# Places of split weights counted among split units, next weights rounded ahead of the residual, and a new order of the mixers' first jobs

## What is computed

```python
for l in range(DEPTH):                      # 2
    x = x + 0.5 * swiglu(rms_norm(x, ffn1_norm[l]), ffn1_w_gate[l], ffn1_w_up[l], ffn1_w_down[l])
    h = rms_norm(x, mix_norm[l])
    (nq, nkc, nvc, ..., wq, wk, wv, bgate) = jnp.split(h @ w_in[l], SPLIT_POINTS, axis=-1)
    y_nsa = nsa_attention(...)              # 8 heads; compressed, selected and window keys
    y_sb = stick_breaking_attention(...)    # 4 heads
    y_swa = swa_sink_attention(...)         # 4 heads
    g = sigmoid(bgate).reshape(B, S, 3, D_MODEL)
    merged = (g[:, :, 0] * (y_nsa @ w_up_nsa[l]) + g[:, :, 1] * (y_sb @ w_up_sb[l])
              + g[:, :, 2] * (y_swa @ w_up_swa[l]))
    x = x + merged @ w_out[l]
    x = x + 0.5 * swiglu(rms_norm(x, ffn2_norm[l]), ffn2_w_gate[l], ffn2_w_up[l], ffn2_w_down[l])
```

## Time and profile before

| | us |
|---|---|
| median of 3 runs | 2611.62 (2607.24 to 2613.82) |
| profiled execution | 2605.64 |
| its span, first to last instruction | 2603.8 |
| PE busy | 2497.8 |
| DVE busy | 1629.0 |
| ACT busy | 1190.7 |
| POOL busy | 367.0 |
| mean granted TensorE clock, of full | 0.979 |

### The profile page before, as it was taken

The page is one execution under the profiler, slowest core; times in us unless marked ns, Lnnn a source line. Parts: engine busy times, 40 slices in busy tenths (PEclk is TensorE's granted clock), DMA queues, the critical chain, the costliest instruction groups (busy, mean ns, idle before and its releaser), DMA issues.

```text
span 2603.8 us, 42299 instructions
## 1 busy us (share of the span) xinstructions
PE 2497.8 (96%) x18041; PEld 2319.9 (89%) x18041; DVE 1629.0 (63%) x2438; ACT 1190.7 (46%) x1950; POOL 367.0 (14%) x385
## 2 busy tenths in 40 slices
PE   8999989999999999999999988999999999999998
PEld 7999978999999898899998655888888999999998
DVE  4787466777887865667774876542443654556753
ACT  5444456544344355555444543431332534344653
POOL 1311000332023000022331220200001011011000
PEclk9999899999999999999999999999999999999999
DMA  7667544567676766347775220233322423334552
GB/s 237 211 220 219 154 135 119 166 223 235 228 233 223 230 154 190 113 126 250 259 262 156 58 68 1 75 104 97 97 98 88 129 90 115 99 108 141 166 195 98
DMA packets 386385, 401.65 MB, mean 154 GB/s; under 512 B 44695, under 2 KB 370611, under 8 KB 385940
## 3 DMA queue, kind: packets, MB, share of 16 engines
q1 hardware_dynamic: 383448, 391.19, 48.1%
q10 hardware_dynamic: 2748, 7.76, 0.8%
HBM read 394.72 MB, written 4.19 MB: 153 GB/s over the span
## 4 chain that ended last, share of the span: by engine, by line
PE 74%; DVE 17%; ACT 5%; issue 2%; DMA 1%; POOL 1%; ACTq 0%; DVEq 0%; SPq 0%
PE bank L672 22%; PE bank L673 21%; PE bank L674 21%; DVE rounded L2332 6%; PE bank L680 3%; DVE plain L2321 3%; ACT rounded L1588 2%; PE bank L685 2%; PE bank L1524 1%; DVE plain L2579 1%; POOL plain L3379 1%; ACT plain L1778 1%; PE bank L1087 1%; PE bank L1117 0%; DVE plain L2456 0%
## 5 line engine op out<-in xcount | busy, mean ns | idle before, releaser
L672 PE MATMUL bank<-rounded 128*128 128x256 f32 (+1 forms) x3704 | 1120.4, 302 | 22.2 <-DVE rounded L2332 17.8
L673 PE MATMUL bank<-rounded 128*128 128x256 f32 (+1 forms) x3704 | 1102.4, 298 | 0.0
L674 PE MATMUL bank<-rounded 128*128 128x256 f32 (+1 forms) x3704 | 1101.7, 297 | 0.0
L2332 DVE TENSOR_TENSOR rounded<-plain,rounded 128x1024 fp32r<-128x1024 f32 (+1 forms) x618 | 722.6, 1216 | 518.9 <-ACT rounded L1588 518.7
L672 PEld LDWEIGHTS bank<-rounded 128*128 128x128 f32 x3704 | 717.5, 194 | 57.2 <-DVE rounded L2332 20.3
L1588 ACT ACTIVATE rounded<-plain 128x1024 fp32r<-128x1024 f32 (+1 forms) x630 | 616.8, 1032 | 327.9 <-PE bank L674 283.7
L673 PEld LDWEIGHTS bank<-rounded 128*128 128x128 f32 x3704 | 717.5, 194 | 16.4
L674 PEld LDWEIGHTS bank<-rounded 128*128 128x128 f32 x3704 | 717.1, 194 | 16.5
L672 PE MATMUL bank<-rounded,rounded 128*128 128x256 f32 (+2 forms) x1472 | 452.6, 307 | 19.9 <-DVE rounded L2332 16.5
L673 PE MATMUL bank<-rounded,rounded 128*128 128x256 f32 (+2 forms) x1472 | 449.9, 306 | 0.0
L674 PE MATMUL bank<-rounded,rounded 128*128 128x256 f32 (+2 forms) x1472 | 448.6, 305 | 0.0
(11 more groups left out here) (306 smaller groups left out, 1988.3 us busy)
## 6 DMA issues: line engine op xcount, KB each, us to landing
plain<-in_mlp_w SPq DMA_DIRECT2D x64, 1024.0 KB, 5.3
plain<-in_ada_w SPq DMA_DIRECT2D x48, 1024.0 KB, 5.4
plain<-in_ffn_w_gate SPq DMA_DIRECT2D x44, 1024.0 KB, 5.8
plain<-in_ffn_w_up SPq DMA_DIRECT2D x44, 1024.0 KB, 5.9
plain<-in_ffn_w_down SPq DMA_DIRECT2D x32, 1024.0 KB, 5.2
plain<-in_w_in SPq DMA_DIRECT2D x32, 1024.0 KB, 5.6
plain<-in_od_w_in SPq DMA_DIRECT2D x32, 1024.0 KB, 5.7
plain<-in_ffn_w_down SPq DMA_DIRECT2D x16, 768.0 KB, 5.1
```

What stands on the lines that cost most here:

```text
L672: pe.matmul(dst, a[0], b[0], start=first and i == 0, stop=False)
L673: pe.matmul(dst, a[0], b[1], start=False, stop=False)
L674: ins = pe.matmul(dst, a[1], b[0], start=False, stop=last and i == n - 1)
L2332: dve.tensor_tensor(low, raw, top, SUB).then_inc(*done(("lo", m, half)))
```

## The change

Three things. First, the split places are handed out by a unit's rank among split units (`split_turn`) and no longer by its number; so `before(m)` is the split unit three ranks back. The raw places stay at m % 3. Second, in the FFN's down projection ACT writes `hi` of the unit three ahead, and the modulation's fill, and DVE writes `lo`, ahead of the residual, its operand for the next product, and the squares. Third, in the mixer, PE's second gate product precedes the compressor's last part, the value product of the compressed branch goes behind gate 2, `third(i)` goes ahead of `compressed(0)`, ACT loads its Exp table by an activation on a spare element, takes job 0's weights ahead of gate 2 and of `headroot`; DVE does `then(0)` right after `first(0)`, `headnorm` after `first(1)`, the gate units' `lo` one iteration later; and the up-projection waits for the bank of the last attention output instead of DVE's mark `attended`, while the last `lo` (unit 71) stands behind that mark.

```diff
     def slot(self, m):
+        return SPLIT + 4096 * (self.split_turn[m] % AHEAD)
     def before(self, m):
-        m -= AHEAD
-        while m >= 0 and self.units[m][2] != "split":
-            m -= AHEAD
-        return m if m >= 0 else None
+        n = self.split_turn[m] - AHEAD
+        return self.split_units[n] if n >= 0 else None
...
         gate(0)
+        gate(1)
         compress(1, 1)
         keyfactors()
-        gate(1)
...
         scores(0)
         gate(2)
+        values_compressed()
         headsum("kc", 15)
...
                 scores(i + 1)
+            gate(4 + 2 * i)
+            third(i)
             if i == 0:
                 compressed(0)
-            gate(4 + 2 * i)
-            third(i)
...
-                for x in new(at(s, "attended", "dve")):
+                for x in new(at("free", s, "ao", n - 1)):
                     pe.wait_ge(*x)
...
         for x in range(12):
             blk, k0 = x // 3, 8 * (x % 3)
+            if x < 11:
+                hi(U[s, "d", blk, k0] + 3)
+                fill(s, 22 + x)
             if k0 == 16:
...
-            if x < 11:
-                hi(U[s, "d", blk, k0] + 3)
-                fill(s, 22 + x)
...
         gate(0)
+        gate(1)
         hidden(1)
-        gate(1)
         headsq("kc", M.bank(s, "kc")[:, 0:15], 15, ("kc",))
+        act.activation(M.spare, M.epsc, ACT.Exp, bias=0.0, scale=1.0).then_inc(*done())
...
+        weights(0)
         gate(2)
-        weights(0)
+        for x in new(at(s, "vc")):
+            act.wait_ge(*x)
+        act.activation(b_.vc[0:15, :, :], grid(M.bank(s, "vc")[0:15, 0:128], c=2), ACT.Copy, scale=1.0).then_inc(
+            *done((s, "vc", "s"), ("free", s, "vc")))
+        hi(U[s, "w1", 1, 1] + 3)
         headroot("kc", 15)
-        hi(U[s, "w1", 1, 1] + 3)
         gate(3)
...
             blk, k0 = x // 3, 8 * (x % 3)
+            if x < 11:
+                lo(U[s, "d", blk, k0] + 3)
             if k0 == 16:
...
             if x < 11:
-                lo(U[s, "d", blk, k0] + 3)
                 fill(s, 22 + x)
...
         first(0)
-        lo(U[s, "bg", 0] + 3)
         then(0)
-        headnorm("kc", b_.kc[:, 0:15], 15)
         lo(U[s, "w1", 1, 1] + 3)
-        lo(U[s, "bg", 1] + 3)
         for i in range(n):
             if i + 1 < n:
                 first(i + 1)
+                if i == 0:
+                    headnorm("kc", b_.kc[:, 0:15], 15)
                 then(i + 1)
+            else:
+                lo(U[s, "bg", 1 + i] + 3)
...
-            lo(U[s, "bg", 2 + i] + 3)
+            if i + 1 < n:
+                lo(U[s, "bg", 1 + i] + 3)
         here(s, "attended", "dve")
         for x in new(at(s, "attended", "pe"), at(s, "attended", "act"), L.last()):
             dve.wait_ge(*x)
+        lo(U[s, "bg", 11] + 3)
```

More of the change, by code:

```diff
@@ L231, in __init__ @@
         self.plan()
+        self.split_units = [m for m, u in enumerate(self.units) if u[2] == "split"]
+        self.split_turn = {m: n for n, m in enumerate(self.split_units)}
     def piece(self, tensors, o, n):
@@ L262, in part @@
     def part(self, m, k, c0, n=128):
-        o = SPLIT + 4096 * (m % AHEAD) + k * self.units[m][3] + c0
+        o = self.slot(m) + k * self.units[m][3] + c0
         return self.split_words(o, n), self.split_words(o + 2048, n)
@@ L269, in halves, with slot @@
     def halves(self, m):
-        width, raw, o = self.units[m][1], self.raw(m), SPLIT + 4096 * (m % AHEAD)
+        width, raw, o = self.units[m][1], self.raw(m), self.slot(m)
         for a, n in ((0, width // 2), (width // 2, width - width // 2)):
             yield raw[:, a:a + n], self.split_words(o + a, n), self.seen(o + a, n), self.split_words(o + 2048 + a, n)
+    def slot(self, m):
+        return SPLIT + 4096 * (self.split_turn[m] % AHEAD)
     def before(self, m):
-        m -= AHEAD
-        while m >= 0 and self.units[m][2] != "split":
-            m -= AHEAD
-        return m if m >= 0 else None
+        n = self.split_turn[m] - AHEAD
+        return self.split_units[n] if n >= 0 else None
     def is_split(self, m):
@@ L1041, in mixer, with values_compressed @@
         ins.then_inc(*done((s, "kc")))
-        b = bank(s, "vc")
-        for x in new(at(s, "hidT", 1, "s")):
-            pe.wait_ge(*x)
-        for g in range(2):
-            ins = plain(b[0:15, g * 64:g * 64 + 64],
-                        [(b_.hidT[1][:, c, g * 15:g * 15 + 15], v2[:, 2 + c, :]) for c in range(2)])
-        ins.then_inc(*done((s, "vc")))
+        def values_compressed():
+            b = bank(s, "vc")
+            for x in new(at(s, "hidT", 1, "s")):
+                pe.wait_ge(*x)
+            for g in range(2):
+                ins = plain(b[0:15, g * 64:g * 64 + 64],
+                            [(b_.hidT[1][:, c, g * 15:g * 15 + 15], v2[:, 2 + c, :]) for c in range(2)])
+            ins.then_inc(*done((s, "vc")))
         def compressed(step):
@@ L1915, in mixer @@
         gate(0)
+        gate(1)
         hidden(1)
-        gate(1)
         headsq("kc", M.bank(s, "kc")[:, 0:15], 15, ("kc",))
-        for x in new(at(s, "vc")):
-            act.wait_ge(*x)
-        act.activation(b_.vc[0:15, :, :], grid(M.bank(s, "vc")[0:15, 0:128], c=2), ACT.Copy, scale=1.0).then_inc(
-            *done((s, "vc", "s"), ("free", s, "vc")))
+        act.activation(M.spare, M.epsc, ACT.Exp, bias=0.0, scale=1.0).then_inc(*done())
         def compressed(step):
@@ L2754, in mixer @@
         lo(U[s, "va", 1] + 3)
+        lo(U[s, "bg", 0] + 3)
         hidden(1)
@@ L2806, in first @@
             n = 128 * (i + 1)
-            landed = [at(s, "vc"), at(s, "gk"), at(s, "T"), at(s, "rq")]
+            landed = [at(s, "cb", 1, 1), at(s, "gk"), at(s, "T"), at(s, "rq")]
             for g in range(2):
```

## The result

| | before | after |
|---|---|---|
| median | 2610.72 us (4 runs, 2607.24 to 2613.82) | 2580.76 us (4 runs, 2577.38 to 2581.84) |
| profiled execution's span | 2603.8 us | 2575.6 us |
| mean granted clock | 0.979 | 0.983 |

The ratio is 0.9885, 95% interval 0.9872 to 0.9897, so 30.0 us (27 to 33) less. The forecast was 2584 with a range of 2574 to 2599. The two spans differ by 28.2 us.

The account below looks back on a forecast made before the run. PE was taken to bound the kernel, with idle time, mostly waits for `lo`, and half clock left to win. Gains of 11.4 + 8 + 5.5 + 2.5 + 0.5 - 0.6 = 27.3 us off 2611.6 gave 2584, range 2574 to 2599.

Parts of the forecast that it names:

- Step 1: End of each mixer's attention: the first up-projection's stall goes, less a bank wait; gain 5.7 us per mixer.
- Step 2: First jobs of each mixer's attention: the new order shortens PE's waits and half clock; gain 4 us per mixer.
- (b): First jobs: `keyfactors` and compressed keys come later; the compressed scores' wait grows from 0.4 to about 1.6 us.
- (a): First jobs: early Exp table and direct `then(0)` ready job 0's weights sooner; waits of 0.89 and 0.4 us go.
- Step 3: Down projection in b0 and b1: `hi` and `lo` ahead of the residual; gain 5.5 and 2.5 us.
- Step 4: Down projection in a0 and a1: same reorder, paid back in bank waits; net -0.6 and +0.5 us.
- Step 5: Split places by rank: PE isn't waiting at the gate and up phase's holds; gain 0.
- A: FFN part gives nothing: b0's and b1's gains go in a0's and a1's bank waits; 2592 us, chance 0.13.
- B: First jobs: compressed keys and gated weights come too late, so that part gives nothing; 2592 us, chance 0.15.
- C: FFNs: residual behind `lo` makes PE wait for a bank at 12 steps; 2655 us, chance 0.03.
- D: b0's holds are by landing, not order, so only the attention-end gain remains; 2600 us, chance 0.09.
- E: Up-projection: `lo` slowed beside POOL's merges, 1.5 us more per mixer; 2587 us, chance 0.10.

Follow-up runs that it names:

- e4: Old kernel with only the up-projection waiting for the last attention output's free bank and the last `lo` behind DVE's mark: 2600.43 us, ratio 0.9970.
- e8: Changed kernel with `headnorm` ahead of `first(1)` and the gated compressed weights in the first job's round, ahead of `lo`: 2572.78 us, ratio 0.9840.
- e11: Changed kernel without the spare-element activation that loads ACT's Exp table early: 2582.98 us, ratio 0.9884.
- e2: Old kernel with only the FFN's new order (`hi`, fill and `lo` ahead of residual and squares), old split places: 2613.93 us, ratio 1.0018.
- e12: Old kernel with the FFN's new order and the new split places together, mixers as before: 2602.96 us, ratio 0.9954.
- e5: Changed kernel with DVE's two residual additions ahead of `lo` in a0 and a1: 2569.91 us, ratio 0.9842.
- e6: e5 with DVE's modulation step of the unit before (k0 = 8) also behind the two residuals: 2572.36 us, ratio 0.9851.
- e9: Changed kernel with the edits of e6 and e8 together: 2560.71 us, ratio 0.9810.
- e1: Old kernel with only the split places by rank, every engine's order as before: 2605.06 us, ratio 0.9978.
- e3: Old kernel with the mixers' new order alone, FFNs and split places as before: 2592.01 us, ratio 0.9935.

## Why the prediction held, point by point

**The view of the bound held.** PE idle for `lo`, by order and not by DVE's load: 34.2 us went to 14.4 with DVE's busy time unchanged (1629.0 and 1629.2). I had said about 13. One reading was off: PE's idle time is 2603.8 - 2497.8 = 106.0 us, not 94; no term used it.

**Step 1, the end of the attention, 5.7 in each mixer.** The stall and its half clock went whole, 6.7 us in m0 and 6.5 in m1. What comes back was undersized: 1.0 (bounds 0 to 2.2), measured 2.6, and it is not a bank wait behind `lo` but PE at w_out reaching the merges of the last chunk. e4 gives it alone, 7.8 us for the 7.9 of the table. My argument of spare time in 453.9 to 473.9 looked at means over 20 us; the last chunk's chain (merges, then ACT's rounding, then DVE's) has no cover.

**Step 2, first jobs, 4 in each.** 5.9 and 4.4. The waits that are left are 0.7, 1.9 and 1.9, 4.5 us and not 5.5. In (b) the place, `headnorm` behind `first(1)`, and the size (1.6) were right, but the victim was another: not the compressed scores but `third(0)`, whose bank is the one that `headnorm` frees (1.93 us, L2631); e8 takes it away by moving that step. In (a) the credit to the table load was wrong by e11; what won those 1.3 us must be the rest, `then(0)` without `lo` before it or job 0's weights ahead of gate 2; no run separates the two. The half clock there fell to 3.5 us in m0 (0.05 x 35 x 2) but stayed near 6.7 in m1 (0.91 over 998 to 1035), which is the difference between the two mixers.

**The drain beside a table load** (the Trainium skill, "ScalarE: Activation LUTs", What ACT_TABLE_LOAD costs: 1.28 and 1.38 us) doesn't show in any trace here. In e11 the load ends at 343.17 and the Exp starts at 344.06, when its maximum is ready; in the earlier trace rows 0.02 us lie between. By these rows the load is 1.28 us and no more.

**Step 3, b0 and b1.** b0's stall and half clock went whole, 6.2 us for a forecast of 5.5. It is the order that wins it: e2 has 5.4 of it with the old places. b1's down projection won 2.0 for 2.5.

**Step 4, a0 and a1.** The sum held, -0.6 and +0.5 against -1.4 and +0.5, and so did its inside: 3.19 us of bank wait in a0 (forecast 3.2), and half clock, which I had given one case in two; 4.79 in a1 (forecast 4.2) and half clock; 1.87 at x/0 (forecast 2.3). That a0 comes so near is in part luck: five kernels have this wait of 3.19 us, three of them with half clock behind it, and over a0 the kernels with the changed FFNs run from 1.4 us lost (the changed kernel) to 1.2 gained (e8, e12). DVE and PE in the changed kernel, in a1:

```profile
879.74 2.36 DVE L2340 TENSOR_TENSOR rounded<-plain,rounded 128x1024 fp32r<-128x1024 f32 x2 [2.27 <-ACT rounded L1595]
882.02 1.28 DVE L2464 TENSOR_REDUCE plain<-bank 128x4 f32<-128x512 f32 x2
...
883.62 1.82 DVE L2340 TENSOR_TENSOR rounded<-plain,rounded 128x768 fp32r<-128x768 f32 x2
885.36 0.42 DVE L2528 SCALAR_TENSOR_TENSOR plain<-bank,plain 128x256 f32<-128x256 f32 x1
...
885.83 0.58 PE L676 MATMUL bank<-rounded,rounded 128*128 128x256 f32 x1 [4.79 <-DVE plain L2528]
```

Two pairs of `lo` and the modulation's reads stand ahead of an addition of 0.42 us for which PE waits. It is the longest wait that the new order makes, and e5, e6 and e9 shorten or remove it.

**Step 5, the places, 0.** This step failed. "PE isn't waiting there" looked at the held `hi` itself; but what it held was DVE's queue, and PE's wait stood one block later (1.20 at 1244.83, and 0.7 twice). e1 gives 5.7 us alone. And in a1 the order without the places costs more than it wins (e2), so places and order are worth 11 us more together than apart. That the total came out right is luck as far as this goes, since the misses offset: b1 2.2 and the first jobs 2.3 too little, the up-projections 3.5 too much.

**The rivals.** A (FFNs give nothing) fell by e12, B (new waits at the first jobs) by e3 less e4, 9.2 us. C had three places, as counted, and no more: PE's wait for the residual's bank appears three times. D fell with b0. E (`lo` slowed beside POOL) was no more than before: in the changed kernel's up-projection one pair takes 2.91 us where the earlier trace rows has 3.35, and the others 2.36.

## What to carry to other kernels

Read a wait on the bounding engine back to what stands ahead of the releaser in its own order: a 0.4 us step that frees a bank belongs ahead of a 2.4 us step that serves something three units away, and a held step on an engine that "has time" can still be paid one block later through the queue behind it. A change of order and a change of buffer assignment are to be tried together as well as apart: here one alone gave 5.7 us, the other alone lost 4.7, and both gave 12.0. When the bounding engine gets through a stretch faster, look at the last step of the helpers' chain behind it, not at their mean load.

## What the runs showed of the hardware

The same wait was followed by different stretches of half clock (the 1.2 GHz level), or by none. PE waits 3.19 us for a bank in a0 in five kernels. At it or right behind it the changed kernel has 6.8 us at half clock (0.63 in its window above), e2 and e11 have 3.4, e8 and e12 have none. The windows of e12 and then of e11 around that wait:

```profile
217.00:227.00 10.00, 6.81 (x57) 6.60 (x56) 4.30 (x10) 3.37 (x7) 1.52 (x2) 1.00 0.71 221
```

```profile
218.00:228.00 10.00, 6.81 (x45) 6.60 (x44) 4.49 (x10) 3.13 (x6) 1.53 (x2) 0.83 0.70 220
```

Shorter waits varied too: the wait of 2.35 us in a0 brought none in the old kernel and 3.4 us in e4 (0.76 over 206 to 213), and the one of 1.87 us at a1's x/0 none in the changed kernel and 3.4 us in e8 (0.72 over 845 to 851). So the prediction's rule, that a stall of 3.2 us or more brings half clock and one of 2.35 does not, held in the one trace that it was read from and does not hold in the others. The 2.6 us with which I priced a stretch is one value among many: beyond itself a wait of 3.19 us cost between nothing and 2.9 us (half of the 5.8 us at half clock that lie behind it in the changed kernel). What decides the length was not tried.

In the first 65 us and in the mixers' projections half clock also came without a long stall before it: in the old kernel's 292 to 320 us PE was busy all 28.00 us, with the clock at 0.87. These places moved from kernel to kernel. That is some 3 us of difference between two traces which no edit explains, so a gain of that size read from one pair of traces is not yet a gain of the edit.
